# A decoder layer with three head groups: fp32 matmuls on parts of the TensorE array become full-width calls, and the order of others changes

## The reference, cut to what matters

```
# gated linear attention, one chunk; b is the running sum of the log decays in the chunk
o      = (q * exp(b)) @ state + causal(scores with decay between positions) @ v
state  = exp(b_last) * state + (k * exp(b_last - b))^T @ v
# cross-attention
p = softmax(q @ mk^T / 8);  y = p @ mv
# layer
x = LN1(alpha * x + concat(y_gla, y_conv, y_xa) @ w_out)
x = LN2(alpha * x + square(relu(x @ w1)) @ w2)
```

## Time and profile before

| | |
|---|---|
| median of 3 runs | 2180.87 us (2177.76 to 2182.1) |
| the profiled execution | 2182.1 us |
| its span, first to last instruction | 2180.4 us |
| PE busy | 2087.3 us, 96% |
| DVE busy | 1380.6 us, 63% |
| ACT busy | 1006.5 us, 46% |
| POOL busy | 532.0 us, 24% |
| mean granted TensorE clock | 0.986 of full speed |

### The profile page before, as it was taken

One profiled execution on the slowest core, in us unless ns is written; L12 is line 12 of the kernel. 1 busy time (PEld: TensorE's weight loads), 2 busy tenths in 40 slices (PEclk: granted clock), 3 DMA queues, 4 the chain that ended last, 5 costly groups with the idle time before them and its releaser, 6 DMA issues.

```text
span 2180.4 us, 28904 instructions
## 1 busy us (share of the span) xinstructions
PE 2087.3 (96%) x11392; PEld 1688.7 (77%) x11392; DVE 1380.6 (63%) x1898; ACT 1006.5 (46%) x1344; POOL 532.0 (24%) x483
## 2 busy tenths in 40 slices
PE   6999999999999999799999999999999999999996
PEld 5677787778777777688887788888788888778884
DVE  3668567756865587556564776676565645964458
ACT  3535454444445446455454654444333333633334
POOL 3002020101110313111010244444594700710004
PEclk9999999999999999899999999999999999999998
DMA  6223333324142514356556778677958555665553
GB/s 195 59 59 94 101 107 117 108 68 163 51 126 59 187 47 135 105 170 212 176 173 225 258 251 283 243 276 271 325 197 284 197 193 193 217 227 193 192 194 135
DMA packets 241063, 374.26 MB, mean 172 GB/s; under 512 B 16368, under 2 KB 117776, under 8 KB 240928
## 3 DMA queue, kind: packets, MB, share of 16 engines
q1 hardware_dynamic: 212096, 272.68, 38.4%
q0 software_dynamic: 28832, 99.74, 13.1%
HBM read 272.74 MB, written 99.61 MB: 171 GB/s over the span
## 4 chain that ended last, share of the span: by engine, by line
PE 51%; DVE 5%; issue 3%; DMA 2%; ACT 2%; POOL 0%; SPq 0%; DVEq 0%; ACTq 0%; POOLq 0%
PE main L68 9%; PE main L70 9%; PE main L69 9%; PE sc L68 6%; PE sc L70 6%; PE sc L69 6%; DVE w_lo L1563 2%; PE aux L70 1%; PE ob L70 1%; PE aux L68 1%; PE ob L68 1%; PE aux L69 1%; PE ob L69 1%; DMA raw<-in_w_ff_dram 1%; ACT x_hi L1499 0%
## 5 line engine op out<-in xcount | busy, mean ns | idle before, releaser
L1563 DVE TENSOR_TENSOR w_lo<-w_b,w_hi 128x1024 fp32r<-128x1024 f32 x144 | 215.7, 1499 | 246.9 <-ACT w_hi L1533 246.7
L1563 DVE TENSOR_TENSOR w_lo<-raw,w_hi 128x1024 fp32r<-128x1024 f32 x144 | 202.5, 1409 | 126.2 <-ACT w_hi L1533 126.1
L1533 ACT ACTIVATE w_hi<-raw 128x1024 fp32r<-128x1024 f32 x144 | 152.5, 1060 | 254.8 <-PE main L70 112.3
L1533 ACT ACTIVATE w_hi<-w_b 128x1024 fp32r<-128x1024 f32 x144 | 152.2, 1057 | 182.6 <-PE aux L70 79.7
L1053 DVE TENSOR_TENSOR w_lo<-raw,w_hi 128x1024 fp32r<-128x1024 f32 x116 | 141.2, 1223 | 141.6 <-ACT w_hi L763 140.7
L68 PE MATMUL main<-xT_lo,w_hi 128*128 128x512 f32 (+1 forms) x528 | 217.3, 412 | 1.5 <-DVE xT_lo L1065 1.5
L69 PE MATMUL main<-xT_hi,w_lo 128*128 128x512 f32 (+1 forms) x528 | 205.6, 389 | 0.0
L70 PE MATMUL main<-xT_hi,w_hi 128*128 128x512 f32 (+1 forms) x528 | 205.5, 389 | 0.0
L68 PE MATMUL sc<-x_lo,w_hi 128*128 128x512 f32 x448 | 177.8, 397 | 13.7 <-DVE x_lo L1506 6.1
L68 PE MATMUL main<-x_lo,w_hi 128*128 128x512 f32 x448 | 175.7, 392 | 7.3 <-ACT z L1884 6.7
L68 PE MATMUL main<-w_lo,w_hi 128*128 128x512 f32 x448 | 175.8, 392 | 4.9 <-DVE w_lo L1563 4.9
(11 more groups left out here) (254 smaller groups left out, 4678.9 us busy)
## 6 DMA issues: line engine op xcount, KB each, us to landing
raw<-in_w_in_dram SPq DMA_DIRECT2D x80, 512.0 KB, 3.7
h_dram<-z SPq DMA_DIRECT2D x64, 512.0 KB, 4.1
raw<-h_dram SPq DMA_DIRECT2D x112, 256.0 KB, 2.7
w_b<-h_dram SPq DMA_DIRECT2D x112, 256.0 KB, 2.7
h_dram<-h_s SPq DMA_DIRECT2D x48, 512.0 KB, 4.5
rows<-in_x_dram POOLq DMA_DIRECT2D x32, 512.0 KB, 5.2
raw<-in_w_out_dram SPq DMA_DIRECT2D x32, 512.0 KB, 3.7
raw<-in_w_ff_dram SPq DMA_DIRECT2D x32, 512.0 KB, 6.7
```

The lines of the kernel that those rows point to most:

```text
L1533: act.activation(ff.w_hi[:, n % RING, :], slot_tile(ff, m), ACT.Copy).then_inc(ff.hi_done, 1)
L1563: dve.tensor_tensor(ff.w_lo[:, n % RING, :], slot_tile(ff, m), ff.w_hi[:, n % RING, :].bitcast(F32), ALU.subtract).then_inc(ff.lo_done, 1)
```

## The change

It has six parts.

1. `score`: the four matmuls of 64x64 with one column each, which sum `gate` over a head's channels, become one call with 128x128 weights and two columns (`head_sum`, ones for the channels of one head in each). Both sums now lie in bank `sc[1]`, columns 448 and 449. The semaphore of `sc[0]` is raised with the last score of head 0. DVE waits for `sc[1]` first and for `sc[0]` behind the two diagonal writes.
2. `attend`: the two state products with 64 weight columns and 128 moving columns become one with 128 weight columns and 256 moving ones. Each head reads its own quarter of the result; the other two quarters are not used.
3. `xattn_score`: both calls of head 0 come before both of head 1, and the wait for head 1's bank stands between them.
4. `xattn_attend`: the eight calls with 64 weight columns and 128 moving columns become four with 128 and 256. They fill all of bank `ob`, and half of it is used.
5. ACT copies `ob` in two instructions of 64 partitions each, with a semaphore for the first (`xy_copied`), for which the two later readers of `xy_raw` wait too.
6. `ones` and `few` are allocated behind `masks` and `w_gate`, among the mixer's tiles; `head_sum` is written by four small memsets on DVE at the start.

```diff
-        ones = sb("ones", [P, P])
-        few = sb("few", [P, 28])
         x_piece = sb("x_piece", [P, 1024])
...
         masks = sb("masks", [P, 6, 2 * 64], U8)
+        ones = sb("ones", [P, P])
         low = sb("low", [P, KT, 2 * RANK], F32R)
         w_gate = sb("w_gate", [2 * RANK, 256])
+        few = sb("few", [P, 28])
...
+        head_sum = few[:, 24:26]
...
-                for part in range(2):
-                    keys = slice(64 * part, 64 * part + 64)
-                    for e in range(2):
-                        head = slice(64 * e, 64 * e + 64)
-                        ins = pe.matmul(sc[e][keys, 448:449], gate[head, hp, CH * c + 64 * part:CH * c + 64 * part + 64],
-                                        ones[head, 0:1], start=True, stop=True)
-                        if part == 1:
-                            ins.then_inc(sc_done[e], 1)
+                            if l == 6 and e == 0:
+                                ins.then_inc(sc_done[0], 1)
+                pe.matmul(sc[1][:, 448:450], gate[:, hp, tok], head_sum[:, :], start=True, stop=True
+                          ).then_inc(sc_done[1], 1)
...
-                for e in range(2):
-                    ins = pe.matmul(aux[64 * e:64 * e + 64, 0:DV], k_dec_rows[:, c, 64 * e:64 * e + 64],
-                                    v_rows[:, c, DV * (2 * hp + e):DV * (2 * hp + e) + DV], start=True, stop=True)
+                ins = pe.matmul(aux[:, 0:2 * DV], k_dec_rows[:, c, :], v_rows[:, c, 2 * DV * hp:2 * DV * hp + 2 * DV],
+                                start=True, stop=True)
...
                 for e in range(2):
                     pe.wait_ge(sc_free[e], SC_USES * t + 2 + SC_XA + 2 * j)
-                for i in range(2):
-                    for e in range(2):
+                    for i in range(2):
                         ins = pe.matmul(sc[e][:, M * i:M * i + M], xqT[64 * e:64 * e + 64, i, P * j:P * j + P],
                                         mkT[64 * e:64 * e + 64, i, :], start=True, stop=True)
-                        if i == 1:
-                            ins.then_inc(sc_done[e], 1)
+                    ins.then_inc(sc_done[e], 1)
...
                 for i in range(2):
                     for m in range(2):
-                        for e in range(2):
-                            ins = pe.matmul(ob[64 * e:64 * e + 64, P * i:P * i + P],
-                                            mv[:, m, P * i + 64 * e:P * i + 64 * e + 64],
-                                            xpT[:, m, P * (2 * i + e):P * (2 * i + e) + P],
-                                            start=(m == 0), stop=(m == 1))
+                        ins = pe.matmul(ob[:, 2 * P * i:2 * P * i + 2 * P], mv[:, m, P * i:P * i + P],
+                                        xpT[:, m, 2 * P * i:2 * P * i + 2 * P], start=(m == 0), stop=(m == 1))
...
                     src = xy_raw[:, i, :]
+                    act.wait_ge(xy_copied, 4 * t + 4)
...
-                    act.activation(xy_raw[:, :, P * j:P * j + P], ob[:, 0:2 * P].rearrange("p (i n) -> p i n", i=2),
-                                   ACT.Copy).then_inc(ob_free, 1)
+                    for e in range(2):
+                        r = slice(64 * e, 64 * e + 64)
+                        src = ob[r, :].rearrange("p (i e n) -> p i e n", i=2, e=2)[:, :, e, :]
+                        ins = act.activation(xy_raw[r, :, P * j:P * j + P], src, ACT.Copy)
+                        if e == 0:
+                            ins.then_inc(xy_copied, 1)
+                        else:
+                            ins.then_inc(ob_free, 1)
...
+                dve.wait_ge(sc_done[1], use)
                 for e in range(2):
-                    dve.wait_ge(sc_done[e], use)
-                    steps.mark(dve.tensor_scalar(probs[:, CH * e:CH * e + CH], ident[:, :], sc[e][:, 448:449],
+                    steps.mark(dve.tensor_scalar(probs[:, CH * e:CH * e + CH], ident[:, :], sc[1][:, 448 + e:449 + e],
                                                  None, ALU.mult))
                 steps.settle()
+                dve.wait_ge(sc_done[0], use)
...
-                                                   scalar=decay_last[r, hp, c:c + 1], in1=aux[r, 0:DV],
+                                                   scalar=decay_last[r, hp, c:c + 1], in1=aux[r, DV * e:DV * e + DV],
...
+            for e in range(2):
+                for h in range(2):
+                    dve.memset(head_sum[64 * e:64 * e + 64, h:h + 1], float(e == h))
```

More of the change, by code:

```diff
@@ L251, in hybrid_layer @@
         xmax_ready, xp_ready = sem("xmax_ready"), sem("xp_ready")
-        act_step, dve_step = sem("act_step"), sem("dve_step")
+        act_step, dve_step, xy_copied = sem("act_step"), sem("dve_step"), sem("xy_copied")
         ff.banks, ff.main_banks, ff.sc_banks = [sc[0], sc[1], ob, aux], main_banks, sc_banks
```

## The result

The changed kernel takes 2208.06 us (median of 4 runs, 2207.6 to 2210.16) where the kernel before took 2179.68 us on the same chip (4 runs, 2177.76 to 2182.1). The ratio is 1.0133, with a 95% interval of 1.0119 to 1.0147: **28.4 us slower**. The forecast was 2195 us with a range of 2187 to 2207. The sign was right, the size was twice what the sum said, and the result lies just above the range.

The account below looks back on a forecast made before the run. The prediction took PE as the bound, busy for 96% of the span. Its terms, 10.5 + 4.8 + 0.1 + 0 - 1.5 = +13.9 us, gave 2196.0 from the profiled 2182.1, forecast as 2195 us, range 2187 to 2207.

Parts of the forecast that it names:

- Cross-attention output: Mixer, 16 calls of xattn_attend: four full-array calls of 256 columns replace eight overlapping half-width ones, +10.5 us.
- lower bound of +8: Low end for the cross-attention output term, if the full-width calls enter at no cost in front of the score.
- Column sums: Mixer, 32 calls of score: one two-column call with unhidden weight loads, +0.15 us a call, +4.8 us in all.
- State product: Mixer, 32 calls of attend: one full call of 256 columns replaces two half-width ones, +0.1 us, within 1.5.
- Scores at 0: Mixer, 16 cross-attention score calls: head-major order changes nothing if instructions for the idle half start past waiting ones, 0 us.
- The rival of a strict order: Cross-attention scores lose their overlap because matmuls keep program order: +10.4 us more, 2205 us in all, chance 0.18.
- ACT's copies at 0: One ACT copy becomes two, +6 us on ACT but covered by its idle time, so 0; at most 6 us.
- What idle time takes back: Mixer: waits before the second transposes in block 0 and attend steps absorb some PE lateness, together -1.5 us.
- The two tiles that move in SBUF: The two moved tiles shift feed-forward tiles by 624 bytes, costed at 0 with +-2 us.
- stretch from 830 us on: The feed-forward part, not edited, 1350 us long; it should keep its length, or the prediction is wrong.
- Faster: Feed-forward tiles' new places in SBUF remove half of that part's 52 us of idle PE: 2169 us, chance 0.05.

Follow-up runs that it names:

- e4: The kernel before with only the wide cross-attention output call and ACT's two copies: 2193.43 us against 2181.37, ratio 1.0051.
- e5: The kernel before with only the column sums of the gate as one call, with DVE's waits and the memsets: 2182.51 us against 2181.37, ratio 1.0007.
- e7: The kernel before with only the state product as one full-array call: 2179.48 us against 2180.32, ratio 0.9998.
- e6: The kernel before with only the new order of the cross-attention scores: 2181.07 us against 2180.32, ratio 1.0.
- e2: The changed kernel with the two tiles `ones` and `few` moved back: 2195.76 us against 2181.37 for the kernel before, ratio 1.0068.
- e1: The kernel before with only the two tiles `ones` and `few` moved: 2194.6 us against 2181.37, ratio 1.0062.
- e3: The changed kernel with an unused tile of 128 bytes ahead of `x_piece`: 2198.53 us against 2180.29 for the kernel before, ratio 1.0077.
- e13: The kernel before with `ones` and `few` moved and an unused tile of 128 bytes ahead of `x_piece`: 2178.7 us against 2181.46, ratio 0.9989.
- e9: The changed kernel with 128 bytes ahead of the weight slots, so everything lies 128 bytes further: 2207.91 us against 2180.29 for the kernel before.

## Why the prediction was right on the sign and short on the size

*Cross-attention output, +10.5 us.* Right: 1.82 and 1.72 us measured where 1.82 and 1.73 were worked out, and e4 alone costs 12.1 us. (Its lower bound of +8 does not follow from its condition: without the 0.09 us in front of 12 scores it is 9.4.)

*Column sums, +4.8 us.* Right for the call (0.16 us, priced 0.15). All of it arrives at the end of the mixer in e5's profile; what reaches the end of the kernel is unclear, between nothing and all of it.

*State product, +0.1 us.* Right, 0.53 us against 0.52; e7 is not to be told from before.

*Scores at 0.* Right. The rival of a strict order (2205 us) is closest to the measured time and still wrong: the score is 1.07 us long in the kernel after and in e6, and e6 costs nothing. Who looked only at the total would have taken it. The order of starts in the earlier trace rows (L548 at 128.96, ahead of L542 at 129.00) and the length in e6 (1.07 us, 264.93 to 266.00) do not agree with a strict order, where the matmuls use different parts of the array.

*ACT's copies at 0.* No wait of PE for `xy_raw` appears in the views of the kernel after. But the wait for ACT's `v_rows` grows by 3.0 us in e4 and by 3.1 in e2 (8.8), so ACT did not come out at nothing. Whether the second copy causes it is not shown: the copies were not tried apart from e4.

*What idle time takes back, -1.5 us.* Right for the two waits that it names: in e2 they give back 1.5 us, and 3.0 after, with the slower main matmuls on top. But in e2 the longer wait for `v_rows` takes it away again, and PE idles in the mixer for 40.8 us, against 39.9 before.

*The step that failed* is "The two tiles that move in SBUF shift feed-forward tiles by 624 bytes; I cost that at 0, with +-2 us". It was mis-sized: the move costs 13.2 us (e1, 9.8 to 17.0). It was also incomplete in two ways. The shift moves not only feed-forward tiles but also the mixer's `xT` and `y` tiles (`xT_hi` from 104576 to 103936, `y_hi` from 71808 to 71168), operands of its main matmuls; and it is 640 bytes (`x_piece` from 51328 to 50688), because `few` takes 128 bytes for its 112. With the exact figure the remainder by 512 changes from 128 to 0. Nothing in the trace of before could give the price, since all of its main matmuls have one difference, but the bound of 2 us had no row behind it. One nanosecond on each of the 2688 matmuls of the expanding half alone is 2.7 us, so a bound should have been worked out from their number. The prediction's test that the stretch from 830 us on stays unchanged in length is the one that failed: the expanding half grew by 9.3 us. The stretch as a whole shows it poorly, 1351.7 us from the mixer's end before and 1356.3 after, since the contracting half was shorter. The rival "Faster", through the new places of the feed-forward tiles, named the right cause with the wrong sign and the wrong mechanism: in the expanding half PE's busy time grew by 12.4 us, and its idle time only went from 16.0 to 12.8.

By the terms of the sum, 13.9 us were forecast, and e2, the change without the move, costs 14.4, with an interval of 10.0 to 19.6. That the two are so close is in part luck. In e2's profile the mixer ends 16.8 us later than before (845.5 against 828.7), which is near the sum of the terms plus the 3.1 us on `v_rows`, 17.0, and the stretches behind it are 4.2 us shorter.

## What to carry to other kernels

When a change allocates, frees or reorders SBUF tiles, work out where every operand of the busiest engine lies afterwards, rounding included, and keep the differences between weight and moving tiles as they were; an unused tile of 128 bytes was worth 10 us (after against e3) to 16 us (e1 against e13) here. Price such a side effect as nanoseconds times the number of instructions that it touches, and look for it in start-to-start distances, in a stretch that nobody edited. When each edit measures as priced and the total does not, divide the total by stretches before choosing a rival that happens to have the right sum.

## What the runs showed of the hardware that was not expected

- In the expanding half the main matmuls, with 512 moving columns, follow each other at 227 ns (means of 226.8) where the places of both slot tiles and the x tiles in SBUF agree in their remainder by 256 bytes, and at 232 to 233 ns (means of 232.4 to 233.3) where they differ by 32, 64 or 128 bytes. The common place itself can be 128 or 256 (contracting half of the kernel before and of e9, 226.9 ns in both). The granted clock was the same in the stretches compared, 0.98 in the expanding half before and in e1.
- 5 ns on the matmul cost 11.5 us in the expanding half of e1, where PE idles for 13.0 of 654.0 us, and 3.3 us in its mixer, where idle time took 5.8 of the 9.2 us.
- In the kernel after, the two weight loads of the call with two moving columns took 0.21 us ahead of main's (129.42 to 129.63), and the one full-width call took 0.16 us more, 0.48 us against 0.32, than four calls on quarter arrays that ran over each other.
- Calls for one half of the array were not held up behind those for the other: the cross-attention scores take 1.06 us in the old order (266.12 to 267.18) and 1.07 us in the new (e6, 264.93 to 266.00), although the new one puts two calls for the same half behind each other.
